# Four groups of matmul operands moved off a common 512-byte grid in SBUF

## The chip, the cores and the metric

The kernel runs on one core of a Trainium2 chip. The metric is the device time of one execution in microseconds (us). Before the change it is 2531.43 us, the median of three runs (2530.93 to 2531.8 us).

## The reference

A stack of transformer layers over 256 tokens of width 2048, in float32:

```python
h = layernorm(x)
for l in range(2):                        # first block
    proj = h @ w_in[l]
    y_mla = latent_attention(proj, w_uq, w_ukv) * silu(gate)   # 8 heads
    y_pool = pooled means @ w_pool * silu(gate)
    y_conv = gated short convolution * silu(gate)
    h = layernorm(ALPHA * h + concat(y_mla, y_pool, y_conv) @ w_out[l] + b_out)
# second block
x = h + 0.5 * (silu(n(h) @ gate1) * (n(h) @ up1)) @ down1      # 5632 features
x = x + concat(forgetting, sliding-window, memory attention of n(x) @ w_in_2) @ w_out_2
x = x + 0.5 * (silu(n(x) @ gate2) * (n(x) @ up2)) @ down2
```

`n` is an RMS norm. The keys and values of the memory attention come from 256 more tokens (`mem`), normed and multiplied by `w_mem_k` and `w_mem_v`.

## The kernel before

**Split operands.** Every weight matrix streams through SBUF in slabs of 128 partitions by 2048 numbers (1 MB). SP loads a slab into one of four places of `raw`. ACT copies it, rounded to the matmul type fp32r, into `high` (L1374), and DVE writes the remainder `raw - high` into `low` (L1787). Both have two places of 8 KB per partition. Features are split in the same way: each tile of 128 features is a row of 512 numbers (2 KB per partition), 256 tokens of the rounded part and behind them 256 tokens of the remainder. These rows stand in `xs` (normed features, 16 rows), `hidden` (feed-forward features, 22 rows at a time), `mixs` (mixed features ahead of an output projection, 16 rows), `memh` (memory tokens, 8 rows at a time), `lats` (normed latents) and `pooled`.

**Two ways to multiply.** In the first (`product`, L932 and L936) a 128x128 block of weights is loaded into the array and the features stream: 512 columns against the block of `high`, then 256 columns against the block of `low`. It serves the regions `in_a` to `in_d`, `uq`, `uk`, `mixout` and `down`. In the second (`product_natural`, L946, L947 and L948) 128 tokens of a feature row are loaded into the array and 512 columns of weights stream:

```python
xh, xl = still[:, b * P:(b + 1) * P], still[:, S + b * P:S + (b + 1) * P]
eng.matmul(bank_, xh, hi, start=start, stop=False)
eng.matmul(bank_, xl, hi, start=False, stop=False)
return eng.matmul(bank_, xh, lo, start=False, stop=stop)
```

It serves `up` (from `xs`), `wide` (from `hidden`), `out` (from `mixs`), `mem` (from `memh`), `nat` and `heads` (from `xs`) and `uv` (from `lats`). TensorE takes all of them in program order, and each matmul has a weight load of its own (PEld), which is issued while the matmul ahead of it streams.

**Places in SBUF.** `at(name, shape, dt, offset)` (L365) gives a tile its address: the next free one, or a given one in a shared area. `raw`, `high`, `low`, `xs`, `x` and the memory tiles follow one another from the start, each a multiple of 4 KB long; then come the shared area `work` (62 KB, in which `hidden`, `mixs`, `lats`, `pooled` and many short-lived tiles begin at whole KB) and a second shared area at `memh_at` (16 KB: `memh`, `mem_b`, and later the tiles of attention and of the feed-forward units). All operands of the fp32r products therefore begin at the same place within 512 bytes, and so do all the blocks cut from them, since a block of 128 numbers is 512 bytes. This is called the grid here. Behind the second area come smaller tiles whose lengths are no multiples of 512 bytes; among them `par` (constants: identity, ones, masks), at 448 bytes past the grid, and `wfs` (the forget gate's weights, 12 numbers of 48 bytes for each row of features), whose blocks begin at 160 + 48 n bytes past it. L1238 multiplies with these: 12 columns are loaded and 512 columns of `xs` stream.

`in_mix` (L684) picks the feature tile of a region. ACT writes the rounded part of the mixed features at L1725 and DVE the remainder at L2218.

Of the kernel before, what the change touches and what calls it, by code (L numbers as in the profile page):

```python
# [7 lines left out]
F32 = mybir.dt.float32  # L8
F32R = mybir.dt.float32r
I32 = mybir.dt.int32  # L10
ALU = mybir.AluOpType
ACT = mybir.ActivationFunctionType
# [3 lines left out]
P = 128  # L16
D = 2048
S = 256
KT = D // P
TB = S // P  # L20
DEPTH = 2
# [11 lines left out]
CT = FT // CHUNKS  # L33
# [136 lines left out]
SPLIT = 2  # L170
# [189 lines left out]
def build(nc, t):  # L360

    with ExitStack() as ctx:
# [9 lines left out]

        raw = at("raw", [P, RAW, 16 * P], F32)
        high = at("high", [P, SPLIT, 16 * P], F32R)
        low = at("low", [P, SPLIT, 16 * P], F32R)

        xs = at("xs", [P, KT, 2 * S], F32R)
        x_at = cursor[0]
# [10 lines left out]
        mem_tok = at("mem_tok", [P, TB, D], F32, work + 20 * KB)  # L389
        square = at("square", [P, KT, S], F32, work + 16 * KB)  # L390
        mixs = at("mixs", [P, KT, 2 * S], F32R, work)
        moment = at("moment", [P, 2 * S], F32, work + 32 * KB)
        moment_sq = at("moment_sq", [P, S], F32, work + 34 * KB)
        rows = at("rows", [P, 3, D], F32, work + 8 * KB)
        z = at("z", [P, TB, D], F32, work + 46 * KB)
        late_moment = at("late_moment", [P, 2 * S], F32, work + 46 * KB)
        wide_sq = at("wide_sq", [P, 2, WIDE_TILES, S], F32, work + 48 * KB)
        hidden = at("hidden", [P, CT, 2 * S], F32R, work)
        lat = at("lat", [P, 8, S], F32, work)
        v_mla = at("v_mla", [P, TB, HEADS * P], F32, work)  # L400
        lats = at("lats", [P, KQ + KKV, 2 * S], F32R, work + 8 * KB)
# [14 lines left out]

        lowsum = at("lowsum", [P, 2, S], F32)
        memh_at = cursor[0]
        memh = at("memh", [P, KT // 2, 2 * S], F32R, memh_at)
        mem_b = at("mem_b", [P, KT // 2, 2 * S], F32, memh_at)  # L420
        wide_turn = at("wide_turn", [P, WIDE_TILES, S], F32, memh_at)
        key_high = at("key_high", [P, S], F32R)
        silu_g = at("silu_g", [P, S], F32)
# [7 lines left out]
        prob = at("prob", [P, 2, TB, S], F32)  # L431
        turned = at("turned", [P, TURNED, TB, S], F32)
        assert cursor[0] == memh_at + 16 * KB
        scale_a = at("scale_a", [P, 2 * S], F32)
        stage = at("stage", [P, TB, 2 * S], F32)
        scale_b = at("scale_b", [P, 2 * S], F32)
# [16 lines left out]
        scale_c = at("scale_c", [P, 2 * S], F32)  # L453
        pos = at("pos", [P, S], I32, work + 38 * KB)
        ang = at("ang", [P, 5, S], F32, work + 39 * KB)
        assert cursor[0] <= nc.sbuf_usable_end, cursor[0] - nc.sbuf_usable_end

        def bank(name, shape):
# [224 lines left out]

        def in_mix(r):  # L684

            return memh if r.name[:3] == "mem" else mixs if r.name[:3] == "out" or r.name == "mixout" else xs

        def wait_added(eng, r, kt):

# [673 lines left out]
        def _(eng):  # L1363
# [220 lines left out]
            def do(kind, *a):  # L1584
# [74 lines left out]
                elif kind == "silu":  # L1659
                    layer, lo, hi = a  # L1660
                    eng.wait_ge(stored, gate_stored(layer, hi - 1))
                    eng.activation(mix[:, lo:hi, :], mix[:, lo:hi, :], ACT.Silu).then_inc(gated, 1)
                elif kind == "normed":
                    c = a[0]
                    if c:
                        eng.wait_ge(head_var, c)
                    for b in range(TB):
                        eng.wait_ge(stored, HEADS_T0 + TB * c + b + 1)
                        for n in range(4):
                            ins = eng.activation((scale_c[:, :], stage[:, 1, :])[b][:, n * P:(n + 1) * P], heads_in(b)[:, n * P:(n + 1) * P], ACT.Square,  # L1670
                                                 accum_out=head_stat[:, 0, 4 * b + n:4 * b + n + 1])
                    ins.then_inc(head_sq, 1)
                    eng.wait_ge(head_var, c + 1)
                    eng.activation(head_stat[:, 2, :], head_stat[:, 1, :], ACT.Sqrt).then_inc(head_root, 1)
                elif kind == "feature":
                    c, half = a
                    pair, gain = pair_of(2 * c + half)
                    eng.wait_ge(head_turned, 2 * c + half + 1)
                    eng.activation(flat(pair), sums[:, :], ACT.Copy, scale=p_(gain)).then_inc(pair_done, 1)
                elif kind == "forget_turn":  # L1680
                    eng.wait_ge(logit_in, 1)
                    eng.activation(fz[:, 2, :, :], fz[:, 1, :, :], ACT.Exp).then_inc(soft_exp, 1)
                    eng.wait_ge(soft_exp, 1)
                    eng.activation(fz[:, 3, :, :], fz[:, 2, :, :], ACT.Ln, bias=1.0).then_inc(soft_ln, 1)
                elif kind == "exps":
                    n = a[0]
                    what, h, _, _, _ = head_spec(n)
                    eng.wait_ge(negmax, TB * (n + 1))
                    for b in range(TB):
                        pr = prob[:, n % 2, b, 0:keys_seen(what, b)]  # L1690
                        eng.activation(pr, pr, ACT.Exp,
                                       bias=stat[:, n % 2, b:b + 1], accum_out=stat[:, n % 2, 2 + b:3 + b])\
                            .then_inc(exps, 1)
                    if what == "swa":

                        eng.activation(stat[:, n % 2, 4:6], stat[:, n % 2, 0:2], ACT.Exp, bias=p_("sinks", h))\
                            .then_inc(sink_exp, 1)
                elif kind == "turn":
                    n = a[0]
                    eng.wait_ge(turns, n + 1)  # L1700
                    if n >= TURNED:

                        eng.wait_ge(mixed, n - TURNED + 1)
                    out_ = turned[:, n % TURNED, :, :]
                    if head_spec(n)[0] == "mem":
                        eng.activation(flat(out_), flat(turn_ps[:, :, :]), ACT.Copy).then_inc(turned_s, 1)
                    else:
                        eng.activation(out_[:, 0, :], turn_ps[:, 0, :], ACT.Copy)
                        eng.activation(out_[:, 1, P:S], turn_ps[:, 1, P:S], ACT.Copy).then_inc(turned_s, 1)
                elif kind == "mix_split":  # L1710
                    layer, c = a
                    at_ = MIX_ORDER[layer].index(c)
                    if layer == DEPTH:
                        eng.wait_ge(head_out, MLA_ALL + (MEM, FOX0, FOX0 + 2, FOX0 + FOX)[c])
                        eng.wait_ge(scores_done, MLA_ALL + (FOX0, FOX0 + 2, FOX0 + FOX, FOX0 + FOX)[c])
                    elif c == 2:

                        eng.wait_ge(stored, REG[f"in_d{layer}"].t0)
                        eng.wait_ge(scores_done, HEADS * (layer + 1))
                        eng.wait_ge(products, REG[f"in_d{layer}"].g0)  # L1720
                    elif c == 3:
                        eng.wait_ge(mix_final, layer + 1)
                    else:
                        eng.wait_ge(head_out, HEADS * (layer + 1))
                    eng.activation(mixs[:, 4 * c:4 * c + 4, 0:S], mix[:, 4 * c:4 * c + 4, :], ACT.Copy).then_inc(mix_h, 1)  # L1725

            def between(name):
                if mix_split(name) is not None:
# [49 lines left out]
        def _(eng):  # L1778
# [208 lines left out]
            def do(kind, *a):  # L1987
# [214 lines left out]
                elif kind == "cum":  # L2202
                    eng.wait_ge(cum_sum, 1)
                    eng.tensor_copy(cum[:, :, :], head_ps[1][:, 0:8 * TB].rearrange("p (b h) -> p b h", b=TB)[:, :, 0:FOX])
                    eng.tensor_copy(cum_rows[0:FOX, :], head_ps[1][0:FOX, S:2 * S]).then_inc(cum_done, 1)
                elif kind == "decay":
                    pair = a[0]
                    eng.wait_ge(decay_sum, pair + 1)
                    eng.tensor_copy(flat(decay[:, 2 * pair:2 * pair + 2, :]), head_ps[1][:, :]).then_inc(decay_done, 1)
                elif kind == "scores":  # L2210
                    shifted_scores(a[0])
                elif kind == "exps":
                    softmax(a[0])
                elif kind == "mix_split":
                    layer, c = a
                    eng.wait_ge(mix_h, 4 * layer + MIX_ORDER[layer].index(c) + 1)
                    w = slice(4 * c, 4 * c + 4)
                    eng.tensor_tensor(mixs[:, w, S:2 * S], mix[:, w, :], mixs[:, w, 0:S].bitcast(F32), ALU.subtract)\  # L2218
                        .then_inc(mix_l, 1)
                elif kind == "mixv":  # L2220
                    n = a[0]
                    what, h, _, _, dest = head_spec(n)
                    eng.wait_ge(mixed, n + 1)
                    if what == "mla":

                        eng.wait_ge(gated, gates_done(n // HEADS, dest))
                        eng.tensor_tensor(mix[:, dest, :], head_ps[n % 2][:, 0:S], mix[:, dest, :], ALU.mult)\
                            .then_inc(head_out, 1)
                    else:
                        eng.tensor_copy(mix[:, dest, :], head_ps[n % 2][:, 0:S]).then_inc(head_out, 1)  # L2230
# [323 lines left out]
```

## Time and profile before

| | |
|---|---|
| median of 3 runs | 2531.43 us |
| span of the profiled execution | 2529.6 us |
| TensorE (PE) busy, matmuls | 2513.3 us, 99%, 12088 matmuls |
| weight loads (PEld) busy | 2107.5 us, 83% |
| VectorE (DVE) busy | 1859.2 us, 73% |
| ScalarE (ACT) busy | 1323.1 us, 52% |
| DMA | 480.84 MB, mean 190 GB/s |

A row of a group gives line, engine, operation, output<-inputs, array rows*columns, shape of what streams, count, busy time and mean duration of one. A matmul's duration includes its way through the array and overlaps with that of the next, so durations of neighbours add up to more than the time that passes. What counts for the span is the distance from one start to the next, called pitch here. In a timeline row that merges n equal instructions, the time given is that from the first start to the last end, so the pitch is (time - duration of one) / (n - 1).

### The profile page before, as it was taken

The numbers are of one execution on the slowest core, as the hardware profiler recorded it, in microseconds if no ns is written. First come the engines' busy times: TensorE is split into PE (matmuls) and PEld (weight loads), VectorE is DVE, ScalarE is ACT, GpSimd is POOL, SyncE is SP. The second block draws the span as 40 slices with busy tenths as digits, with TensorE's granted clock in tenths as the row PEclk, the third lists the DMA queues.
The fourth block names the chain that finished last, engine by engine and source line by source line (L and its number), as shares of the span: only waits on it lengthen the run. The fifth ranks groups of instructions, "written<-read, shape, count | busy, mean of one in ns | idle before, by whom it ended". The sixth has DMA issues, their size and how long they took to land.

```text
span 2529.6 us, 33116 instructions
## 1 busy us (share of the span) xinstructions
PE 2513.3 (99%) x12088; PEld 2107.5 (83%) x12088; DVE 1859.2 (73%) x2991; ACT 1323.1 (52%) x1893; POOL 25.5 (1%) x24
## 2 busy tenths in 40 slices
PE   8999999999999999999999999999999999999999
PEld 6888888888888888888888887888888888888888
DVE  8787658787658777677777786678777767777766
ACT  6675565566566444444444455765544444444443
POOL 4000000000000000000000000000000000000000
PEclk9999999999999999999999999999999999999999
DMA  7555556455555555555555554444555555555554
GB/s 303 202 195 175 192 183 237 168 193 182 186 182 196 187 198 191 192 184 203 195 195 180 192 201 151 146 160 173 184 199 193 190 184 198 200 197 188 196 183 150
DMA packets 71231, 480.84 MB, mean 190 GB/s; under 512 B 8000, under 2 KB 10688, under 8 KB 17216
## 3 DMA queue, kind: packets, MB, share of 16 engines
q1 hardware_dynamic: 71104, 479.16, 53.4%
q8 instruction: 78, 1.28, 0.2%
q14 instruction: 49, 0.40, 0.0%
HBM read 475.72 MB, written 2.10 MB: 189 GB/s over the span
## 4 chain that ended last, share of the span: by engine, by line
PE 83%; DVE 1%; ACT 1%; issue 0%; ACTq 0%; DVEq 0%
PE acc L946 12%; PE acc L948 12%; PE acc L947 12%; PE score L946 10%; PE score L948 10%; PE score L947 10%; PE acc L932 8%; PE acc L936 4%; PE score L932 1%; PE score L1285 1%; DVE low L1787 0%; PE head_ps L1310 0%; PE score L936 0%; PE turn_ps L1294 0%; PE head_ps L1311 0%
## 5 line engine op out<-in xcount | busy, mean ns | idle before, releaser
L1787 DVE TENSOR_TENSOR low<-raw,high 128x1024 fp32r<-128x1024 f32 (+2 forms) x912 | 1079.5, 1189 | 460.2 <-ACT high L1374 451.5
L1374 ACT ACTIVATE high<-raw 128x1024 fp32r<-128x1024 f32 (+2 forms) x912 | 934.7, 1028 | 842.5 <-PE acc L948 435.9
L932 PE MATMUL acc<-xs,high 128*128 128x512 f32 x1184 | 393.4, 395 | 1.5 <-DVE xs L2331 1.2
L946 PE MATMUL acc<-high,xs 128*128 128x512 f32 x928 | 366.3, 395 | 0.3 <-DVE scale_a L1880 0.3
L948 PE MATMUL acc<-low,xs 128*128 128x512 f32 x928 | 361.6, 390 | 0.0
L947 PE MATMUL acc<-high,xs 128*128 128x512 f32 x928 | 361.1, 389 | 0.0
L936 PE MATMUL acc<-xs,low 128*128 128x256 f32 x1184 | 297.5, 278 | 0.0
L946 PE MATMUL score<-high,xs 128*128 128x512 f32 x736 | 286.4, 389 | 0.0
L948 PE MATMUL score<-low,xs 128*128 128x512 f32 x736 | 286.3, 389 | 0.0
L947 PE MATMUL score<-high,xs 128*128 128x512 f32 x736 | 286.3, 389 | 0.0
L932 PEld LDWEIGHTS acc<-xs,high 128*128 128x128 f32 x1184 | 219.2, 188 | 49.6 <-DVE xs L2331 1.9
L1834 DVE STREAM_TRANSPOSE unit_turn<-unit_prod 32x128 f32<-32x128 f32 x704 | 212.8, 302 | 9.8
L936 PEld LDWEIGHTS acc<-xs,low 128*128 128x128 f32 x1184 | 211.8, 188 | 3.9
L948 PEld LDWEIGHTS acc<-low,xs 128*128 128x128 f32 x928 | 174.2, 188 | 36.8
L946 PEld LDWEIGHTS acc<-high,xs 128*128 128x128 f32 x928 | 174.3, 188 | 36.4 <-issue 1.0
L947 PEld LDWEIGHTS acc<-high,xs 128*128 128x128 f32 x928 | 174.3, 188 | 35.5
L948 PEld LDWEIGHTS score<-low,xs 128*128 128x128 f32 x736 | 138.2, 188 | 28.7
L946 PEld LDWEIGHTS score<-high,xs 128*128 128x128 f32 x736 | 138.2, 188 | 28.7
L947 PEld LDWEIGHTS score<-high,xs 128*128 128x128 f32 x736 | 138.2, 188 | 28.6
L947 PE MATMUL score<-high,hidden 128*128 128x512 f32 x352 | 136.9, 389 | 0.0
L946 PE MATMUL score<-high,hidden 128*128 128x512 f32 x352 | 136.9, 389 | 0.0
L948 PE MATMUL score<-low,hidden 128*128 128x512 f32 x352 | 136.9, 389 | 0.0
(410 smaller groups left out, 3200.4 us busy)
## 6 DMA issues: line engine op xcount, KB each, us to landing
raw<-w_up_dram SPq DMA_DIRECT2D x176, 1024.0 KB, 4.8
raw<-w_in_dram SPq DMA_DIRECT2D x76, 1024.0 KB, 4.9
raw<-w_wide_dram SPq DMA_DIRECT2D x75, 1024.0 KB, 4.8
raw<-w_out_dram SPq DMA_DIRECT2D x32, 1024.0 KB, 4.8
raw<-w_heads_dram SPq DMA_DIRECT2D x20, 1024.0 KB, 4.8
raw<-w_mixout_dram SPq DMA_DIRECT2D x16, 1024.0 KB, 4.8
raw<-w_mem_dram SPq DMA_DIRECT2D x8, 1024.0 KB, 4.8
raw<-w_first_dram SPq DMA_DIRECT2D x8, 1024.0 KB, 4.8
```

The source lines that it names most:

```text
L932: return eng.matmul(bank_, hi, moving, start=start, stop=False)
L936: return eng.matmul(bank_[:, 0:S], lo, moving[:, 0:S], start=False, stop=stop)
L946: eng.matmul(bank_, xh, hi, start=start, stop=False)
L947: eng.matmul(bank_, xl, hi, start=False, stop=False)
L948: return eng.matmul(bank_, xh, lo, start=False, stop=stop)
L1285: last = eng.matmul(score[n % 2][:, b, 0:w], qc[:, b * P:(b + 1) * P], kc[:, 0:w], start=(m == 0), stop=(m == len(qk) - 1))
L1374: eng.activation(high[:, s % SPLIT, to:to + n * P], raw[:, s % RAW, at_:at_ + n * P], ACT.Copy).then_inc((highs_a, highs_b)[piece], 1)
L1787: eng.tensor_tensor(low[:, s % SPLIT, w], raw[:, s % RAW, at_:at_ + n * P], high[:, s % SPLIT, w].bitcast(F32), ALU.subtract).then_inc((lo ...
L1834: ins = eng.transpose(to[QUAD * j:QUAD * (j + 1), n, :, :, :], from_[QUAD * n:QUAD * (n + 1), j, :, :, :])
```

## The change

No instruction is added or taken away; addresses differ. `hidden` begins 16 bytes later. The mixed features of the two `out` projections go to a new tile `mixs_out`, 32 bytes past `mixs` (which is kept for `mixout`); ACT's copy and DVE's subtraction write to the one or the other. `memh` and `mem_b` begin 256 bytes later, and all tiles behind that area move up by 256 bytes. `low` leaves its place behind `high` and goes to the end of the allocation, to an address 32 bytes past the grid; `xs` and what follows move down by its 16 KB. `raw`, `high`, `xs`, `mixs`, `lats` and `pooled` stay on the grid.

```diff
-        low = at("low", [P, SPLIT, 16 * P], F32R)
...
         mixs = at("mixs", [P, KT, 2 * S], F32R, work)
+        mixs_out = at("mixs_out", [P, KT, 2 * S], F32R, work + 32)
...
-        hidden = at("hidden", [P, CT, 2 * S], F32R, work)
+        hidden = at("hidden", [P, CT * 2 * S + 8], F32R, work)[:, 4:4 + CT * 2 * S].rearrange("p (k s) -> p k s", k=CT)
...
-        memh = at("memh", [P, KT // 2, 2 * S], F32R, memh_at)
-        mem_b = at("mem_b", [P, KT // 2, 2 * S], F32, memh_at)
+        memh = at("memh", [P, KT // 2, 2 * S], F32R, memh_at + 256)
+        mem_b = at("mem_b", [P, KT // 2, 2 * S], F32, memh_at + 256)
...
         assert cursor[0] == memh_at + 16 * KB
+        cursor[0] += 256
...
+        cursor[0] += (x_at + 32 - cursor[0]) % 512
+        low = at("low", [P, SPLIT, 16 * P], F32R)
...
-            return memh if r.name[:3] == "mem" else mixs if r.name[:3] == "out" or r.name == "mixout" else xs
+            return memh if r.name[:3] == "mem" else mixs_out if r.name[:3] == "out" else mixs if r.name == "mixout" else xs
...
-                    eng.activation(mixs[:, 4 * c:4 * c + 4, 0:S], mix[:, 4 * c:4 * c + 4, :], ACT.Copy).then_inc(mix_h, 1)
+                    to = mixs if layer == DEPTH else mixs_out
+                    eng.activation(to[:, 4 * c:4 * c + 4, 0:S], mix[:, 4 * c:4 * c + 4, :], ACT.Copy).then_inc(mix_h, 1)
...
-                    eng.tensor_tensor(mixs[:, w, S:2 * S], mix[:, w, :], mixs[:, w, 0:S].bitcast(F32), ALU.subtract)\
+                    to = mixs if layer == DEPTH else mixs_out
+                    eng.tensor_tensor(to[:, w, S:2 * S], mix[:, w, :], to[:, w, 0:S].bitcast(F32), ALU.subtract)\
                         .then_inc(mix_l, 1)
```

## Rows read from the trace of the kernel before

**Rows 1.** Summary page, whole span: busy time by engine, and chain by engine

```profile
span 2529.6 us, 33116 instructions
PE 2513.3 (99%) x12088; PEld 2107.5 (83%) x12088; DVE 1859.2 (73%) x2991; ACT 1323.1 (52%) x1893; POOL 25.5 (1%) x24
PEclk9999999999999999999999999999999999999999
...
PE 83%; DVE 1%; ACT 1%; issue 0%; ACTq 0%; DVEq 0%
```

**Rows 2.** Waits of the PE rows alone: who waited, total us, times, longest

```profile
PE sums L1355 <- DMA x_tok<-x_dram: 6.4, 1, 6.4
PE acc L946 <- DVE branch L1906: 2.6, 2, 1.7
```

**Rows 3.** Groups by line and form: count, busy us, mean ns, idle before

```profile
L948 PE MATMUL acc<-low,xs 128*128 128x512 f32 x928 | 361.6, 390 | 0.0
...
L948 PE MATMUL score<-low,xs 128*128 128x512 f32 x736 | 286.3, 389 | 0.0
...
L948 PE MATMUL score<-low,hidden 128*128 128x512 f32 x352 | 136.9, 389 | 0.0
L948 PE MATMUL acc<-low,hidden 128*128 128x512 f32 x308 | 119.8, 389 | 0.0
...
L947 PE MATMUL acc<-high,mixs 128*128 128x512 f32 x256 | 99.6, 389 | 0.0
```

**Rows 4.** The same groups, weights in the array: rows, columns, shape, count

```profile
L932 PE MATMUL acc<-xs,high 128*128 128x512 f32 x1184 | 393.4, 395 | 1.5 <-DVE xs L2331 1.2 <-DVE low L1787 0.2
...
L932 PE MATMUL acc<-mixs,high 128*128 128x512 f32 x224 | 76.8, 394 | 0.0
...
L932 PE MATMUL acc<-hidden,high 128*128 128x512 f32 x88 | 29.6, 393 | 0.0
```

**Rows 5.** Timeline of PE in the first down projection: start us, duration us

```profile
1074.71 0.39 PE L948 MATMUL acc<-low,hidden 128*128 128x512 f32 x1
...
1076.07 0.39 PE L948 MATMUL acc<-low,hidden 128*128 128x512 f32 x1
```

**Rows 6.** Timeline of PE in `mixout`, weights in the array: start us, duration us

```profile
1739.61 0.40 PE L932 MATMUL acc<-mixs,high 128*128 128x512 f32 x1
...
1743.08 0.40 PE L932 MATMUL acc<-mixs,high 128*128 128x512 f32 x1
```

**Rows 7.** Chain of the span, PE pieces: start us, us from piece to piece

```profile
1729.66 1.86 PE acc L932 x8
1731.53 0.95 PE acc L936 x8
...
2496.07 1.81 PE acc L932 x8
```

**Rows 8.** Timeline of PE, the twelve-column matmuls: start us, union us, count

```profile
1535.34 3.88 PE L1238 MATMUL head_ps<-xs,wfs 128*12 128x512 f32 x16
```

**Rows 9.** Their line: duration ns min/median/max, first and last start us

```profile
L1238 PEld LDWEIGHTS head_ps<-xs,wfs x16: 91/92/95, 1535.1 to 1538.6; 128*12 128x12 f32 x16
L1238 PE MATMUL head_ps<-xs,wfs x16: 388/396/398, 1535.3 to 1538.8; 128*12 128x512 f32 x16
```

**Rows 10.** Timeline of PE in a head of attention, plain f32 operands

```profile
177.76 0.59 PE L1310 MATMUL head_ps<-turned,v_mla 128*128 128x256 f32 x2
...
178.41 0.49 PE L1294 MATMUL turn_ps<-par,prob 128*128 128x128 f32 x3
```

**Rows 11.** Lines of these matmuls: duration ns min/median/max

```profile
L1310 PE MATMUL head_ps<-turned,v_mla x32: 377/377/378, 177.8 to 656.1; 128*128 128x256 f32 x32
...
L1294 PE MATMUL turn_ps<-par,prob x100: 270/272/273, 164.8 to 1718.5; 128*128 128x128 f32 x100
```

**Rows 12.** Summary page, splitting of the weights on DVE and ACT

```profile
L1787 DVE TENSOR_TENSOR low<-raw,high 128x1024 fp32r<-128x1024 f32 (+2 forms) x912 | 1079.5, 1189 | 460.2 <-ACT high L1374 451.5
L1374 ACT ACTIVATE high<-raw 128x1024 fp32r<-128x1024 f32 (+2 forms) x912 | 934.7, 1028 | 842.5 <-PE acc L948 435.9
```

## The prediction

> **What bounds the kernel now.** I read the summary page first. TensorE has a matmul under way for 2513.3 us of 2529.6 us, at the full granted clock in every slice, and 83% of the chain that ended last is its own [rows 1]. Next came the waits of TensorE. The longest is the start (6.4 us for the first input), and the next is 2.6 us in two times [rows 2]. So nothing feeds TensorE late. The kernel is as long as its matmuls take one after the other, and only their pitch can change the time. The profiled execution has a span of 2529.6 us, 1.8 us below the median of the runs (2531.4 us); I take differences from the trace and apply them to the median.
>
> **The pitch.** A natural triple (L946, L947, L948) takes 0.68 us: L948 of one triple starts at 1074.71 us and that of the second triple after it at 1076.07 us [rows 5], so 1.36 / 6 = 226.7 ns for each matmul of 512 columns. At 2.4 GHz, the level that a granted clock of 1.0 stands for, this is 544 cycles: 32 more than the 512 columns. With the weights in the array, ten pairs of 512 and 256 columns pass between 1739.61 and 1743.08 us [rows 6], 347 ns a pair or 833 cycles for 768 columns: again 32 more for each matmul. Eight 512-column matmuls of `down` in a row take 1.81 us (226 ns each), and eight in `mixout` take 1.86 us (232.5 ns each), where the eight of 256 columns behind them take 0.95 us (119 ns each, 285 cycles) [rows 7]. So nearly every fp32r matmul in this kernel pays about 32 cycles (13.3 ns) on top of its columns, with all operands on the grid. With some 11,400 such matmuls that is 152 us of the span (an estimate from these pitches). The change can only matter if that surcharge, or the excursions above it, depends on where the operands begin.
>
> **Does plain f32 pay it?** L1310 loads 128 columns and streams 256, twice in 0.59 us with 377 ns for one [rows 10, 11]: a pitch of 215 ns, as long as 512 columns at full clock plus 3 cycles. Its operands are on the grid too. I read plain f32 as two cycles a column. So where the stream asks for half as many numbers a cycle, there is hardly a surcharge. The transposes, with the identity in `par` off the grid, have (0.49 - 0.272) / 2 = 109 ns [rows 10, 11]. That is 2 x 128 columns at full clock (107 ns) and 2 ns more: for plain f32 being off the grid costs no more than being on it.
>
> **The one place off the grid.** L1238 loads 12 columns of `wfs`, 160 + 48 n bytes off the grid, and streams 512 columns of `xs`. Sixteen take 3.88 us at 395 ns for one [rows 8, 9]: (3.88 - 0.395) / 15 = 232 ns, 45 cycles above the columns. Its loads last 92 ns. A load with a tenth of the columns, off the grid, is followed by a longer pitch, not by a shorter one.
>
> **The change part by part.**
>
> *What is the same.* Each engine has the same instructions, waits and order, and each queue the same transfers. No step is moved. DVE writes `low` and ACT writes the mixed features at other addresses. Should these writes take longer, they are covered: in a natural region a slab is 48 matmuls (10.9 us) against two of L1787 (1189 ns each) and two of L1374 (1028 ns each), and with weights in the array it is 16 pairs (5.5 us) against the same four. DVE stands idle for 460 us before L1787, most of it waiting for ACT, which for its part waits for TensorE [rows 12]. So a few per cent on these writes cost nothing. If that cover were gone, each 10 ns on L1787 would cost 912 x 10 ns = 9 us.
>
> *Which matmuls see another relation.* While a matmul streams, the load for the next one runs. What may count is the start of the loaded block less the start of the streamed one, modulo 512 bytes; before the change it is 0 everywhere. After it, in natural triples (while L946, L947 and L948 stream): from `xs` 0, 0, -32; from `hidden` 16, 16, -16; from `mixs_out` 32, 32, 0; from `memh` 256, 256, 224. In pairs with the weights in the array (while 512 and while 256 columns stream): 32 and 0, for `hidden` 16 and -16.
>
> *How many.* `xs` natural: 928 + 736 = 1664. `hidden` natural: (352 + 308) x 3 = 1980. Mixed: 256 x 2 = 512 [rows 3]. 512-column matmuls with `high` in the array: 1184 + 224 + 88 = 1496 [rows 4]. Together 5652; small groups that I leave out (`memh`, `lats`, the `score` groups of the pairs) hold some 450 more. The 3328 matmuls L946 and L947 from `xs` keep their relation.
>
> *Price of one, from both sides.* No row has an fp32r product at another relation with a full load. The best that I can bound is that the surcharge goes altogether, down to the 215 ns of plain f32: -11.7 ns. The worst is a rhythm like that of L1238 or of the eight in `mixout`: 232.5 - 226.7 = +5.8 ns. Nearest to the affected matmuls in kind is the steady 226.7 ns itself, which is in between. I take a quarter of the bounded gain, -2.9 ns. Plain f32 shows that the surcharge isn't in every matmul, so a part may be two streams meeting. But the load passes 128 columns while 256 stream, so the two drift apart by 512 bytes within each load, and an offset of 16 or 32 bytes moves where they meet more than whether they meet. The quarter is a choice, with no row of its own. The sum: 5652 x 2.9 ns = 16.4 us, 2531.4 - 16.4 = 2515.0 us.
>
> The page SBUF — State Buffer of the Trainium skill ("Who interferes with whom") gives TensorE two independent read ports, one for the moving operand and one for weight loads. By that rule the load can't slow the stream, the change does nothing, and the time is 2531 us. The surcharge of 13 ns, which is missing with plain f32, neither proves nor refutes it. The same page ("Door 1", on cachelines) puts SBUF's lines at 16 bytes. A loaded block of 512 bytes has 32 of them, and the surcharge is 32 cycles; that coincidence would speak for a cycle lost to each line loaded. L1238 speaks against it in this trace: its loads read 3 lines, and it pays 45 cycles.
>
> **The rivals.**
>
> *A, part of the surcharge goes (my forecast): 2515 us.* For it: the surcharge isn't universal (plain f32), and the pitch isn't always at its steady value (232.5 ns in one run of eight, 226 in another with the same shapes), so the loads and the streams do react to each other. Against: L1238.
>
> *B, all of it goes where the relation isn't zero: 5652 x 11.7 ns = 66 us, 2465 us.* The relation 0 would be a locked collision that any offset breaks. For it: every operand is on the same grid, and the steady value is exact to a cycle. Against: L1238, off the grid and slow. Also the drift within a load.
>
> *C, nothing: 2531 us.* The 32 cycles belong to each fp32r matmul and not to addresses. For it: the value is the same for 512 and 256 columns, for features or weights in the array, and for all tiles. The skill's rule on read ports would be its reason. It is also the case in which the change doesn't do what it says, since 3328 natural matmuls from `xs` and all 256-column ones but 88 keep relation 0 anyway.
>
> *D, slower: 5652 x 5.8 ns = 33 us, 2565 us.* The steady rhythm at 226.7 ns would be what equal starts bring about; a relation that changes from matmul to matmul (0, 0, -32 in each triple; 32, 0 in each pair) would keep it from settling, as with L1238, whose relation changes each time. The place is the pairs and triples above; it decides as soon as the disturbance outlasts one matmul. If only the 1496 pairs and the 1664 triples from `xs` are hit, it is 18 us, 2550 us.
>
> **How the numbers follow.** A 0.33, B 0.14, C 0.31, D 0.22. This kernel's measurement can tell about 0.2% (5 us) from no change. Faster by more is A and B, 0.47; within 0.2% is C, 0.31; slower by more is D, 0.22. The predicted time is that of A, 2515 us. The range goes from just below B to the milder half of D: 2464 to 2550 us. It leaves out what of B lies beyond its own figure, and about half of D, some 0.15. Both signs hold much of the chance; A's own range is 2500 to 2525 us (1 to 5.5 ns off each affected matmul).
>
> **What the profile after would show.** Counts stay at 12088 matmuls. Under A or B the distance between two L948 of `hidden` falls below 0.68 us, while that of L946 and L947 from `xs` stays; under B it goes to 3 x 215 ns = 0.645 us. With `high` in the array the pair would fall from 347 ns. Under C all of these are the same to 0.01 us. Under D pairs or triples lengthen, and the runs of eight in `mixout` lie above 1.86 us. DVE and ACT rows of L1787, L1374 and L1725 should keep their durations within 2%, and TensorE's waits should stay near 10 us in total. The prediction is wrong if the pitch of matmuls whose relation is still 0 changes too, which would mean that the relation is not what counts, or if TensorE begins to wait for DVE.

## The result: slower by 1.5%, and the profile after

The changed kernel takes 2568.52 us (median of 4 runs, 2568.36 to 2568.79) against 2531.27 us before (4 runs): 37 us more, ratio 1.0148, 95% interval 1.0134 to 1.0162. The forecast was 2515 us. The figure of rival D, 2565 us, was 3.5 us too low.

The summary page of the changed kernel, line numbers moved by three to five:

```profile
span 2566.6 us, 33136 instructions
PE 2550.2 (99%) x12088; PEld 2107.6 (82%) x12088; DVE 1860.1 (72%) x2991; ACT 1325.9 (52%) x1893; POOL 25.3 (1%) x24
PEclk9999999999999999999999999999999999999999
...
L1791 DVE TENSOR_TENSOR low<-raw,high 128x1024 fp32r<-128x1024 f32 (+2 forms) x912 | 1080.2, 1189 | 491.8 <-ACT high L1377 485.2
L1377 ACT ACTIVATE high<-raw 128x1024 fp32r<-128x1024 f32 (+2 forms) x912 | 935.5, 1029 | 876.8 <-PE acc L951 455.6
```

Against [rows 1, 12]: the same 12088 matmuls at the same granted clock, and TensorE is busy 36.9 us longer in a span that is 37.0 us longer. DVE and ACT do their splitting in the same time for each instruction and stand idle for 32 and 34 us more. So nothing reaches TensorE later; its own matmuls are further apart. Its waits say the same (compare [rows 2]):

```profile
PE sums L1358 <- DMA x_tok<-x_dram: 6.1, 1, 6.1
PE acc L949 <- DVE branch L1910: 2.6, 2, 1.6
```

The timeline of PE in the first down projection of the changed kernel, L951 being L948 of before:

```profile
1088.95 0.40 PE L951 MATMUL score<-low,hidden 128*128 128x512 f32 x1
...
1090.35 0.39 PE L951 MATMUL score<-low,hidden 128*128 128x512 f32 x1
...
1092.43 0.39 PE L951 MATMUL score<-low,hidden 128*128 128x512 f32 x1
```

Five triples lie between the first and the last: 3.48 / 5 = 0.696 us a triple, 232 ns a matmul, against 0.68 us and 226.7 ns [rows 5].

A quicker view of pitch counts the matmuls that are under way in a fixed stretch. Columns: stretch, its length, PE busy (x matmuls), granted clock, DMA share, GB/s. In the kernels here the first stretch lies in `out0` (mixed features, natural triples), the second in `up10` (`xs`), the third in `wide10` (`hidden`; in the slowest kernel its first few us are still `xs`), all three without a pause. Two of the count stick out over the ends, so pitch = length / (count - 2). Before:

```profile
290.00:370.00 80.00, 80.00 (x355) 1.00 0.60 210
830.00:1010.00 180.00, 180.00 (x796) 1.00 0.55 192
1030.00:1130.00 100.00, 100.00 (x442) 1.00 0.55 195
```

After:

```profile
290.00:370.00 80.00, 80.00 (x344) 1.00 0.60 208
830.00:1010.00 180.00, 180.00 (x779) 1.00 0.53 187
1030.00:1130.00 100.00, 100.00 (x433) 1.00 0.53 184
```

Before it is 226.6, 226.7 and 227.3 ns. After it is 233.9 ns from `mixs_out`, 231.7 ns from `xs` and 232.0 ns from `hidden`. From the starts of all matmuls of the two traces, triples from `xs` went from 681 to 694 ns, from `hidden` from 680 to 696, from the mixed features from 680 to 700 and from `memh` from 683 to 696. With 1664, 660, 256 and 64 triples that is 22 + 10 + 5 + 1 = 38 us, the whole loss. Pairs with the weights in the array did not lengthen (from `xs` 347.6 before, 347.3 ns after).

One line decides against the bookkeeping of the prediction. From `xs`, the matmuls after the change have 228, 231 and 235 ns for L949, L950 and L951. The second has relation 0, as before the change, and still lost 4.5 ns. If one counts instead by the operands of the matmul that starts next, it is the third whose relation stayed 0, and it lost 8 ns. So a matmul doesn't pay by its own relation alone, whichever way the relation is assigned.

### The profile page after: what moved, and what is told of

It reads as the page before. It is cut to its first block, busy times and chain, and to the rows that moved or that the text cites. A ratio compares the mean times of both kernels' runs of the same rounds, so it can differ in the third digit from the quotient of the medians.

```text
span 2566.6 us, 33136 instructions
## 1 busy us (share of the span) xinstructions
PE 2550.2 (99%) x12088; PEld 2107.6 (82%) x12088; DVE 1860.1 (72%) x2991; ACT 1325.9 (52%) x1893; POOL 25.3 (1%) x24
## 4 chain that ended last, share of the span: by engine, by line
PE 97%; DVE 1%; ACT 0%; issue 0%; ACTq 0%; DVEq 0%
PE acc L951 14%; PE acc L950 14%; PE acc L949 14%; PE acc L935 14%; PE score L951 10%; PE score L950 10%; PE score L949 10%; PE acc L939 7%; PE score L935 1%; PE score L1288 1%; PE score L939 1%; PE head_ps L1313 1%; PE turn_ps L1297 0%; PE head_ps L1314 0%; DVE low L1791 0%; PE sums L1231 0%
## 5 line engine op out<-in xcount | busy, mean ns | idle before, releaser
L951 PE MATMUL acc<-low,xs 128*128 128x512 f32 x928 | 367.5, 396 | 0.0
L949 PE MATMUL acc<-high,xs 128*128 128x512 f32 x928 | 367.0, 395 | 0.2 <-DVE scale_a L1884 0.2
L950 PE MATMUL acc<-high,xs 128*128 128x512 f32 x928 | 365.2, 393 | 0.0
L951 PE MATMUL score<-low,xs 128*128 128x512 f32 x736 | 291.5, 396 | 0.0
L950 PE MATMUL score<-high,xs 128*128 128x512 f32 x736 | 289.6, 393 | 0.0
L949 PE MATMUL score<-high,xs 128*128 128x512 f32 x736 | 287.3, 390 | 0.0
L950 PEld LDWEIGHTS acc<-high,xs 128*128 128x128 f32 x928 | 174.1, 188 | 41.8
L949 PEld LDWEIGHTS acc<-high,xs 128*128 128x128 f32 x928 | 174.2, 188 | 40.2 <-issue 0.7
L951 PEld LDWEIGHTS acc<-low,xs 128*128 128x128 f32 x928 | 174.2, 188 | 38.3
L950 PEld LDWEIGHTS score<-high,xs 128*128 128x128 f32 x736 | 137.9, 187 | 34.1
L949 PEld LDWEIGHTS score<-high,xs 128*128 128x128 f32 x736 | 138.1, 188 | 32.2
L951 PEld LDWEIGHTS score<-low,xs 128*128 128x128 f32 x736 | 138.2, 188 | 30.4
L950 PE MATMUL score<-high,hidden 128*128 128x512 f32 x352 | 139.3, 396 | 0.0
L949 PE MATMUL score<-high,hidden 128*128 128x512 f32 x352 | 139.2, 395 | 0.0
L951 PE MATMUL score<-low,hidden 128*128 128x512 f32 x352 | 137.6, 391 | 0.0
```

## The experiments

Theories ahead of the first four. *Distance*: what matters is the relation, the start of what is loaded less the start of what streams, modulo 512 bytes. *Change*: what matters is that the relation changes from one matmul to the next. *Absolute*: what matters is where a single operand begins. A fourth theory is that the place of `low` in the allocation matters; several runs have it at the end of the allocation and on the grid, and test that. No run leaves work out. Each kernel is the one before the change with the moves named; a diff shows only some of its lines. The ratio is to runs of the kernel before on the same chip. A matmul is called free here when it has the pitch of before, 226.7 ns, and the rhythm at that pitch is called settled.

### Which part costs, and whether the relation is what counts

**`low` alone.**

```diff
-        low = at("low", [P, SPLIT, 16 * P], F32R)
...
+        cursor[0] += (x_at + 32 - cursor[0]) % 512
+        low = at("low", [P, SPLIT, 16 * P], F32R)
```

> Only `low` moves, to the end of the allocation and 32 bytes past the grid; `hidden`, the mixed features and the memory rows stay on the grid. Distance theory (a load whose start differs from the start of what streams costs more) and change theory (only a relation that changes from matmul to matmul costs): every natural triple now has the relations 0, 0, -32, which cost 14 ns a triple from `xs` in the changed kernel; 1664 + 660 + 256 + 64 + 16 = 2660 triples x 14 ns = +37 us, 2569 us. If instead the cost hangs on the tile that is moved, only `xs` triples pay: 1664 x 14 ns = +24 us, 2555 us.

2567.95 us, ratio 1.0144 (1.0128 to 1.0161): all but half a microsecond of the loss. The three stretches:

```profile
290.00:370.00 80.00, 80.00 (x347) 1.00 0.60 210
830.00:1010.00 180.00, 180.00 (x779) 1.00 0.54 190
1030.00:1130.00 100.00, 100.00 (x434) 1.00 0.54 189
```

`hidden` and the mixed features, which did not move, are at 232 ns as well. The cost isn't in the tile that moves but in the triple.

**The features alone** (`hidden` + 16, `mixs_out` + 32, `memh` + 256; `low` at the end, on the grid).

```diff
+        cursor[0] += (x_at + 0 - cursor[0]) % 512
+        low = at("low", [P, SPLIT, 16 * P], F32R)
```

> `hidden` + 16, `mixs_out` + 32, `memh` + 256 as in the change, but `low` (at the end of the allocation) on the grid: the relation is constant within each triple (16, 16, 16; 32, 32, 32; 256, 256, 256) and 0 for `xs`. Distance theory: triples from `hidden`, `mixs_out`, `memh` above 690 ns, those from `xs` at 680 ns; 980 triples x 15 ns = +15 us, 2546 us. Change theory: all triples at 680 ns, 2531 us. `xs` away from 680 ns would say that the place of `low` in the allocation matters by itself.

2536.44 us, 1.0020 (1.0010 to 1.0029).

```profile
290.00:370.00 80.00, 80.00 (x345) 1.00 0.59 206
830.00:1010.00 180.00, 180.00 (x796) 1.00 0.55 193
1030.00:1130.00 100.00, 100.00 (x443) 1.00 0.56 195
```

Neither theory as it stood. A constant 32 costs (80 / 343 = 233.2 ns from `mixs_out`), so it is not only the change of relation. A constant 16 (`hidden`) and a constant 256 (`memh`, 227.4 to 228.2 ns by its starts, as before) are free. `xs` has its old count, so `low` at the end of the allocation does no harm.

**Everything moved by 32 bytes.**

```diff
-        cursor = [(nc.sbuf_base + 31) // 32 * 32]
+        cursor = [(nc.sbuf_base + 31) // 32 * 32 + 32]
```

> All tiles 32 bytes further on, relations all 0 as before. Distance and change theory: 2531 us, triples at 680 ns. If it is the absolute start of an operand that costs (a block that begins inside some larger line): triples above 690 ns, +37 us or more, 2569 us.

2531.53 us, 1.0000 (0.9991 to 1.0010), the counts of before in all three stretches. That rules out the absolute theory for 32 bytes.

**`high` and `low` both at + 32.**

```diff
+        cursor[0] += 32
         high = at("high", [P, SPLIT, 16 * P], F32R)
         low = at("low", [P, SPLIT, 16 * P], F32R)
+        cursor[0] += 480
```

> `high` and `low` both 32 bytes past the grid, all features on it: the relation is -32 throughout in natural triples and +32 throughout in pairs. Distance theory: all 2660 triples lengthen, by 14 ns or more each, 2569 us or more, and the pairs may too. Change theory: nothing changes its relation within a region, 2531 us.

2586.83 us, 1.0219 (1.0202 to 1.0237): 55 us, the most of all runs, with a relation that never changes within a region.

```profile
290.00:370.00 80.00, 80.00 (x345) 1.00 0.58 201
830.00:1010.00 180.00, 180.00 (x773) 1.00 0.53 187
1030.00:1130.00 100.00, 100.00 (x431) 1.00 0.54 184
```

All tiles are at 233.3 ns, which at 2.4 GHz is 560 cycles, 48 above the columns where 226.7 ns is 32 above. The change theory is out; the distance theory holds for 32. The pairs lengthen here too, from 347.6 to 350.7 ns from `xs` by their starts.

### Which distances

**Constant 48, 64, 128** (`hidden` + 48, `mixs_out` + 64, `memh` + 128, `low` on the grid).

```diff
+        mixs_out = at("mixs_out", [P, KT, 2 * S], F32R, work + 64)
...
+        hidden = at("hidden", [P, CT * 2 * S + 24], F32R, work)[:, 12:12 + CT * 2 * S].rearrange("p (k s) -> p k s", k=CT)
```

> `low` on the grid; `hidden` + 48, `mixs_out` + 64, `memh` + 128: constant relations. Theory of a repeating distance (the cost depends on the relation modulo 64 bytes, free near 0, 6.6 ns a matmul at 32): 64 and 128 are free (226.7 ns); 48 is as far from a multiple of 64 as 16, which was free, so `hidden` is free as well: 2531 us. Rival, the cost falls off only with a large distance (256 free, 32 dear): `hidden` at 233 ns gives 1980 x 6.6 ns = +13 us, `mixs_out` +5 us, 2549 us. A second rival: some relation is better than 0 and goes below 226.7 ns.

2550.65 us, 1.0075 (1.0059 to 1.0092).

```profile
290.00:370.00 80.00, 80.00 (x344) 1.00 0.58 206
830.00:1010.00 180.00, 180.00 (x796) 1.00 0.54 192
1030.00:1130.00 100.00, 100.00 (x431) 1.00 0.52 184
```

48 and 64 cost as much as 32 (100 / 429 = 233.1 and 233.9 ns), and `memh` at 128 has 232.4 ns by its starts. A repeat every 64 bytes is refuted; the rival's 2549 us came true.

**Constant -16, 16, 192** (`hidden` + 496, `mixs_out` + 16, `memh` + 192).

```diff
+        hidden = at("hidden", [P, CT * 2 * S + 248], F32R, work)[:, 124:124 + CT * 2 * S].rearrange("p (k s) -> p k s", k=CT)
```

> `low` on the grid; `hidden` + 496 (relation -16), `mixs_out` + 16, `memh` + 192. Repeating distance of 64 bytes: all free, 226.7 ns, 2531 us. If the sign matters (the load ahead of the stream is free, the load behind it is dear): `hidden` at 233 ns, +13 us, 2544 us.

2537.20 us, 1.0022 (1.0012 to 1.0032). `hidden` at -16 is free (x443), but `mixs_out` at 16 is not (x345, 233.2 ns), where `hidden` at 16 had been. The same distance gave two answers. `memh` at 192 is in between (230 ns by its starts).

**`low` alone at 64, and at 16.** The edit is that of the first run with another number; for 16, the tile is cut from one that is 32 bytes longer.

> As the run with `low` alone, but 64 instead of 32 bytes past the grid: relations 0, 0, -64 in every triple, 64 and 0 in pairs. Repeating distance of 64 bytes: nothing, 2531 us. If any change of the relation from one matmul to the next costs: as with 32 bytes, 2568 us.

2570.06 us, 1.0152 (1.0136 to 1.0169).

> `low` alone, 16 bytes past the grid: relations 0, 0, -16. Repeating distance: constant 16 was free, so nothing, 2531 us. If a change of the relation costs by itself, at least part of the 37 us: 2540 to 2568 us. In the changed kernel `hidden` with 16, 16, -16 took 696 ns a triple, which speaks for a cost of the change from 16 to -16, a distance of 32.

2572.04 us, 1.0159 (1.0142 to 1.0176), against the expectation of the repeating distance and dearer than 32 and 64. By the starts, its natural triples take 696 ns, as with 64 bytes; what it takes beyond that run is in the pairs from `xs`, 349.1 ns against 347.0. Relations 0, 0, -16 cost all tiles, with 16 as good as free for `hidden` while it stays constant. So the change within a triple does matter, besides the distance.

**`low` alone at 256.**

> `low` alone, 256 bytes past the grid: 0, 0, -256 in triples. A constant relation of 256 was free for `memh`. Value theory (each matmul pays by its own relation): free, 2531 us. Rhythm theory (matmuls settle to 226.7 ns only while the relation stays the same from one to the next; any change in every triple keeps them near 231 to 233 ns, whichever matmul it falls on): 2568 us or a little more.

2531.30 us, 1.0000 (0.9991 to 1.0009).

```profile
290.00:370.00 80.00, 80.00 (x354) 1.00 0.59 210
830.00:1010.00 180.00, 180.00 (x795) 1.00 0.54 192
1030.00:1130.00 100.00, 100.00 (x443) 1.00 0.55 193
```

A relation that jumps between 0 and 256 in each triple is free, against the rhythm theory as written, which had counted 0 and 256 as different.

**`high` and `low` at 256.**

> `high` and `low` both 256 bytes past the grid: relation -256 throughout natural triples, 256 throughout pairs. Rhythm theory with 256 as a value that settles: 2531 us, triples 680 ns, pairs 347 to 348 ns. If 256 settled for `memh` only by how its short runs are entered: triples near 700 ns, 2586 us, as with 32 bytes.

2531.24 us, 1.0000 (0.9990 to 1.0009), the counts of before. 256 bytes are as good as none, in triples and in pairs: of the distances tried, 0 and 256 alone are free in every run that has them.

### How much each part of the change costs

**`hidden` + 16 and `memh` + 256 alone.**

> Only `hidden` + 16 and `memh` + 256; `low` (at the end) and the mixed features on the grid. Account theory (37 us from `low`, the 5 us of the run with the features alone from `mixs_out` alone): all triples at 226.7 ns a matmul, 2531.4 us within 0.1%.

2531.16 us, 0.9999 (0.9990 to 1.0008). With the run of the features alone, `mixs_out` is the whole of its 5 us: 256 triples x 20 ns. Account of the change: `low` 37 us; once `low` has unsettled everything, the other three together add 0.6 us (2568.52 less 2567.95); alone, `mixs_out` costs 5 and the other two nothing.

### Why 16 bytes give two answers

**`high` and `low` both at + 16.** Both are cut from one longer tile.

```diff
+        both = at("both", [P, 2 * SPLIT * 16 * P + 8], F32R)
+        high = both[:, 4:4 + SPLIT * 16 * P].rearrange("p (k s) -> p k s", k=SPLIT)
+        low = both[:, 4 + SPLIT * 16 * P:4 + 2 * SPLIT * 16 * P].rearrange("p (k s) -> p k s", k=SPLIT)
+        cursor[0] += 480
```

> `high` and `low` both 16 bytes past the grid: relation -16 throughout natural triples. `hidden` settled at +16 and at -16, `mixs_out` at +16 did not. If 16 bytes settle wherever the runs are long: `xs` and `hidden` at 226.7 ns, at most +7 us from the rest, 2531 to 2538 us. If it hangs on how a run is entered, `xs` may stay near 233 ns: 1664 triples x 20 ns = +33 us, 2565 us or more.

2568.33 us, 1.0146 (1.0130 to 1.0161). `xs` and also `hidden`, free at -16 in the earlier run, have 231.7 ns by their starts. The difference between the two is what ran ahead of `hidden`: `xs` at 226.7 ns there, `xs` at 231.7 ns here. The next two runs test that.

**`xs` alone at + 32.** Relation 32 in `up`, 0 in `wide` right behind it.

```diff
+        cursor[0] += 32
         xs = at("xs", [P, KT, 2 * S], F32R)
+        cursor[0] += 480
```

> Only `xs` moves, 32 bytes past the grid: relation 32 throughout its natural triples, 0 for all other tiles. Rhythm theory: `xs` triples near 700 ns (1664 x 20 ns = +33 us), and those of `hidden`, which follow them without a pause, fall back to 226.7 ns a matmul because relation 0 settles from any state: 2531 + 33 = 2564 us. If a rhythm once lost stays lost: `hidden` above 230 ns as well, +10 us or more on top, 2574 us or more.

2562.30 us, 1.0122 (1.0105 to 1.0139). The stretches of `xs` and `hidden`:

```profile
830.00:1010.00 180.00, 180.00 (x773) 1.00 0.53 187
1030.00:1130.00 100.00, 100.00 (x443) 1.00 0.54 188
```

And the chain where the one passes into the other (start us, us to the next piece), four of its pieces, three matmuls apart (a piece begins 0.16 us behind the start of its matmul, so the distances are those of the starts):

```profile
1023.64 0.23 PE acc L948
...
1024.34 0.23 PE score L948
...
1025.03 0.23 PE score L948
...
1025.71 0.23 PE score L948
```

From 1023.64 (`xs`) to 1024.34 us (the first of `hidden`) the triple takes 0.70 us; the triples after it take 0.69 and 0.68 us. By the starts, the first matmul of `hidden` has 231 ns and every one of the 23 behind it 226 or 227, in each of the four places where `hidden` follows `xs`. So relation 0 finds the short pitch from the long one, here within one matmul. It isn't always as quick. In the kernel before, where a run of natural matmuls begins behind plain f32 matmuls or behind pairs, the matmuls behind the first swing between 224 and 236 ns, and it is mostly the fourth to the eleventh that begins the rhythm of 226 and 227 ns, with every operand on the grid. `mixs_out` at 16 begins behind such a start and stays at 233.3 ns, where `mixs` at 0 comes down to 226.7.

**`xs` at + 32 and `hidden` at + 16.**

> `xs` + 32 and `hidden` + 16. `hidden` at 16 was free where the triples ahead of it ran at 226.7 ns. Entry theory (at 16 the settled rhythm holds if it is there on entry, and is not found otherwise): `hidden` now near 231 to 233 ns, 660 triples x 15 to 20 ns = +10 to 13 us over the run with `xs` alone, 2574 to 2577 us. Value theory (16 is free for `hidden`, whatever went before): the same as with `xs` alone, 2564 us.

2575.39 us, 1.0175 (1.0158 to 1.0192), 13.1 us above the run with `xs` alone.

```profile
830.00:1010.00 180.00, 180.00 (x774) 1.00 0.53 187
1030.00:1130.00 100.00, 100.00 (x430) 1.00 0.53 184
```

`hidden` at 16 now has 100 / 428 = 233.6 ns (233.3 by the starts), where the same tile at the same relation had 226.7 ns behind a settled `xs` (x443). 660 triples x 20 ns = 13 us, as the entry theory said. At 16 bytes the short pitch lasts if it is there on entry, and isn't found otherwise.

All mean pitches of a natural matmul in ns, by relation (from the starts of all matmuls of the run named):

| relation | pitch | run |
|---|---|---|
| 0 throughout | 226.7 | before, all moved by 32 |
| 256, or 0 and 256 in turn | 226.7 | weights or `low` at 256 |
| 16 or -16, entered at 226.7 | 226.7 | `hidden` + 16, + 496 |
| 16 or -16, entered otherwise | 231.7 to 233.3 | `mixs_out` + 16, weights + 16, `xs` + 32 with `hidden` + 16 |
| 32, -32, 48, 64 throughout | 233.3 | weights or `xs` + 32, `hidden` + 48, `mixs_out` + 64 |
| 0, 0, -16 | 232.0 | `low` + 16, from `xs` |
| 0, 0, -32 | 231.7 | `low` + 32, from `xs` |
| 0, 0, -64 | 232.0 | `low` + 64, from `xs` |

None is below 226.7 ns, and none of the 14 kernels beats the kernel before.

In the pairs the sign of the relation can count too. By the starts, pairs from `xs` take 350.7 ns at + 32 (weights + 32) and 347.4 ns at -32 (`xs` + 32), against 347.6 before. The 88 pairs from `hidden` take 353.0 ns at + 16 (`hidden` + 496) and 346.9 ns at -16 (`hidden` + 16), against 346.6 before, but 346.8 ns at + 32. They are too few to show in the time, and no rule comes out of these values.

### Whose operands count

No run was made for this question, but the seams of the run with `hidden` at 48 bear on it. There `xs` is at 0, `hidden` at 48, and all weights are on the grid. Start and duration of the last matmul of one and the first of the other, where `xs` passes into `hidden` and where `hidden` passes back:

```profile
1022.64 0.40 PE L951 MATMUL acc<-low,xs 128*128 128x512 f32 x1
1022.88 0.40 PE L949 MATMUL score<-high,hidden 128*128 128x512 f32 x1
...
1145.85 0.39 PE L951 MATMUL acc<-low,hidden 128*128 128x512 f32 x1
1146.07 0.39 PE L949 MATMUL score<-high,xs 128*128 128x512 f32 x1
```

The last matmul from `xs`, whose own operands are both on the grid, already has the long pitch: 232 or 233 ns by the starts, in all four such places. The last one from `hidden`, whose own loaded operand is at 48, has the short pitch: 226 or 227 ns, in all three. So the time from one start to the next goes by what is loaded for the next matmul, and not by what the running one was loaded with.

## Why the prediction was wrong, step by step

**What bounds the kernel: right.** The span grew by what TensorE's busy time grew, with the same matmuls, clock and waits. The writes of `low` and of the features did not slow, as said.

**How much cover the writes had: misread.** The prediction gives a slab 48 natural matmuls. A slab holds four stretches of 512 columns, each multiplied by two blocks of tokens with three matmuls, so it is 24, or 5.4 us. The trace agrees: in 100 us of `hidden`, with 442 matmuls under way, DVE splits 37 half slabs (a half slab is 1024 numbers wide).

```profile
L1787 DVE TENSOR_TENSOR low<-raw,high x41: 691/1225/1227, 1029.5 to 1129.6; 128x1024 fp32r<-128x1024 f32 x33, 128x512 fp32r<-128x512 f32 x8
```

The two subtractions of a slab take 2.4 us, so the cover holds all the same, and nothing came of the slip.

**How many matmuls: the wrong unit.** I counted 5652 matmuls by whether their own relation changed, and left out 3328 from `xs` that keep relation 0. They pay too: L949 and L950 from `xs` went from 227 to 228 and 231 ns. That is what the prediction had named as proof against itself (the pitch of matmuls at relation 0 changes). And the 1496 with `high` in the array, which I counted in, paid nothing. Two errors of opposite sign; the right unit is the natural triple, 2644 of them (and 16 from `lats`).

**The price of one: the failed step.** The forecast took a gain of 2.9 ns, a quarter of the way to plain f32, "with no row of its own". It came out as a loss of 4 to 7 ns for each natural matmul, by tile, to 231.4 to 233.3 ns by the starts. The rows there were pointed up: L1238, off the grid, at 232 ns [rows 8, 9], and the eight of `mixout` at 232.5 ns [rows 7]. They pointed without proving: by the starts, the 512-column matmuls of the pairs have 232 ns before the change too, on the grid, and those of 256 columns 116 ns, so the "32 more for each matmul" is right for the pair only on average. I had read 226.7 ns as 512 columns and a surcharge that a change could lift. The runs show it as the better of two rhythms, which the common grid holds in place. Its being exact to a cycle and the same for all tiles was a sign of a steady rhythm, but not of which one: with the weights at 32 all tiles are at one pitch too, 233.3 ns. The forecast never asked whether it had the better or the worse one in front of it.

**Rival D: right in sign and in the kind of cause, near in size partly by luck.** It said that equal starts bring about the steady rhythm and that relations that differ keep it from settling, at + 5.8 ns on 5652 matmuls, 33 us. Measured: 37 us over 7932 natural matmuls, 4.7 ns each on average. Its count was the one above, with 1496 matmuls that paid nothing and without 3328 that paid, so a price too high met a count too low. Its reason, a relation that changes from matmul to matmul, is one half: a constant 32 is worse still.

**Rivals B and C.** B (a locked collision that any offset breaks) is refuted: no run has natural matmuls below 226.7 ns. C, with the rule of the Trainium skill's page SBUF — State Buffer ("Who interferes with whom") that TensorE's two read ports are independent, would have given 2531 us. The measured 37 us, from addresses alone, don't fit that rule as it stands for fp32r operands: what is loaded and what streams do depend on each other here. The same page's 16-byte lines ("Door 1") do not explain the values either: a shift by whole lines (16, 32, 64 bytes) costs, and one by 256 does not.

**The range** ended at 2550 us and cut D in half; with a bound from two rows at + 5.8 ns it should have reached D's own 2565 us and beyond.

**Slips of the sums.** None moves the forecast. The pitch of L1310 by the rows is 0.59 - 0.377 = 213 ns; the 215 ns in the text is the value by the starts, and is four cycles above 512 columns, not three. D's own sum, 2531.4 + 32.8, gives 2564 us.

## What to carry to other kernels

Where TensorE is the bound, look at the distance from start to start, not at durations: a pitch that is the same everywhere can be one of several steady rhythms, and the question is what holds it there, before asking what it costs. For fp32r products with a load for each matmul, keep all operands at one place modulo 256 bytes, which cost nothing in any run here; `low` alone, off by 16 to 64 bytes and used in a third of the matmuls, slowed its neighbours too. And take a price from the nearest measured row, here the one operand that was off the grid already, rather than from a bound that no row comes near.

## What the runs showed of the hardware, and what stays open

- An fp32r matmul of 512 columns with its own 128-column load repeats each 226.7 ns (544 cycles at 2.4 GHz) in one state and, with the operands a constant 32, 48 or 64 bytes apart, each 233.3 ns on average (560 cycles) in the other. The state hangs on addresses. Between them lie 3% of the pitch and 2.2% of this kernel: 2531 to 2587 us.
- There is memory in it: at a relation of 16 bytes the same tile runs at 226.7 or 233.3 ns, by the state in which its region is entered.
- Pairs of 512 and 256 columns with the weights in the array react less: 347.1 to 350.7 ns over all runs, from `xs`.
- Moving all operands together by 32 bytes changes nothing (2531.53 us).

Open: what inside TensorE or SBUF makes the two states. That the load for the next matmul and the running stream get in each other's way fits all runs and the seams above, but isn't shown. The seams leave a second reading, that the load counts against what the next matmul itself streams, since `high` and `low` begin at the same place modulo 512 bytes there. Whether distances that are no multiple of 16 bytes, or constant ones between 64 and 256 other than 128 and 192, do better wasn't tried.
